# Head norms in a six-layer kernel: two tiles' means and spreads issued side by side on two halves of TensorE's array, and modulation blocks in a changed order

## The chip, the cores and the metric

The kernel runs on one core of a Trainium2 chip. The metric is device time in microseconds of one execution. All matrix products are in f32; the trace shows each of them as two MATMUL records (two passes over the moving operand), so "x4" in a row of the trace is two matmuls.

## What is computed

A chain of transformer layers on one sequence of 512 tokens (model width 1024), with a context of 256 tokens beside it. The first two layers (A/B and C/D) mix several kinds of attention; the next four have modulated norms, a mixer each and an MLP. What matters here is that queries and keys are normalised head by head before attention, and that the four later layers are modulated by vectors made from a condition:

```python
def rms_norm(z, g):
    zf = z.astype(jnp.float32)
    y = zf * lax.rsqrt(jnp.mean(zf * zf, axis=-1, keepdims=True) + NORM_EPS)
    return (y * g.astype(jnp.float32)).astype(z.dtype)
...
    qa = apply_rope(rms_norm(heads(qa, A_HEADS), a_qk_norm[0]), cos, sin)
    ka = apply_rope(rms_norm(heads(ka, A_KV_HEADS), a_qk_norm[1]), cos, sin)
...
def ada_mods(vec, w, b):
    m = jax.nn.silu(vec) @ w + b
    return [mi[..., None, :] for mi in jnp.split(m, N_MOD, axis=-1)]
```

## The kernel before, in words

Activations lie transposed: 128 features on the partitions, tokens along the free axis (512 for the sequence, 256 for the context). A stage of kind "project" walks over blocks of weights. A block is 2 MB, lies in one of three slots of `ring`, and is loaded on the SP queue in a fixed order: block b waits until block b-3 has been used (`freed_by`). For each tile of a block TensorE makes K/128 matmuls (L1395), ScalarE or VectorE takes the result out of PSUM, and then the list `t.after` of that tile is played: side steps that every engine plays in the same order, each doing its own part. So the order of all work is written out by hand in `after` lists.

A head norm (class `Heads`, one job for up to ten tiles) is made of such side steps. A tile holds 128 features, two heads of 64 (or four of 32). `square` (ScalarE, L1944) squares the tile into one of two buffers; the next square into the same buffer waits until `mean` has read it. `mean` (TensorE, L1422) multiplies the squares with a constant 128x22 matrix: each tile adds its two rows to one PSUM bank of 22 rows. After the last tile `sd` takes the root (ScalarE, L1952) and the reciprocal (VectorE, L2402). `spread` (TensorE, L1433) multiplies the 22 rows with a 22x128 constant, which copies a tile's rows back over its 128 partitions, into one of two banks; VectorE multiplies the tile by it (L2414). `swap` (TensorE, L1450) permutes features for the rotation, which VectorE (L2428, L2432) and GpSimd finish.

A modulation block is a 2 MB block of `in_ada_w` in the same ring ("ride"). VectorE sums it over its rows, weighted with the condition (L2277, L2281: 16 instructions for two conditions, 8 for one), into the buffer `partial`. One ride later TensorE adds up the partitions with matmuls of one column (`modulation`, L1355, 8 matmuls for two conditions), and VectorE adds the bias (`mods`, L2264). `ride(a)` is called by TensorE and by VectorE at the end of each group of tiles: it finishes the pending block, then takes a. Twelve blocks belong to a layer. In the C/D stage one group rides block X just before two groups that have weights but no tiles (`cmp_w`), and the group behind these, columns 1536 to 2048, rides another, called Y here.

Of the kernel before, what the change touches and what calls it, by code (L numbers as in the profile page):

```python
# [21 lines left out]
P = 128  # L22
D = 1024
KD = D // P
S = 512
C = 256
ST = S // P
HD = 64
# [27 lines left out]
PAIR_TILES, PAIR_ROWS = 11, 22  # L56
CD_PAIR_TILES = 8
QUAD_TILES, QUAD_ROWS, LAT_ROWS = 3, 12, 2
# [32 lines left out]
def head_norm_constants(tiles, rows, segments):  # L91
# [7 lines left out]
    return np.concatenate([mean.reshape(P, -1), spread.reshape(P, -1)], 1)  # L99


def constants():
    pos = np.arange(S)
    out = {}
# [24 lines left out]
    out["hn_pair"] = head_norm_constants(PAIR_TILES, PAIR_ROWS, [(0, 64), (64, 128)])  # L129

    mean, spread = np.zeros((P, 3, LAT_ROWS), np.float32), np.zeros((P, 3, P), np.float32)
    for i, (row, n) in enumerate(((0, 256), (0, 256), (1, 128))):
        mean[:, i, row], spread[row, i] = 1.0 / n, 1.0
    out["hn_cd"] = np.concatenate([head_norm_constants(QUAD_TILES, QUAD_ROWS, [(32 * j, 32 * j + 32) for j in range(4)]),
# [69 lines left out]
class Heads:  # L204


    def __init__(self, tiles, n, consts, rows, parts, swap, cos, sin, wk, mean, spread, turn, counts):
        self.tiles, self.n, self.consts, self.rows, self.parts = tiles, n, consts, rows, parts
# [3 lines left out]
        self.rs = wk[0:rows, 2 * S:2 * S + n]  # L212
# [5 lines left out]
        self.normed = [i for i, t in enumerate(tiles) if t[1] is not None]  # L218
# [10 lines left out]
def build_program(nc, dram, out_dram, stages_kept=10000):  # L229
    ctx = ExitStack()  # L230
    with ctx:
# [200 lines left out]
        def residual_halves(src, op, arg, normed, rides=0, **kw):  # L432
# [22 lines left out]
            return stage("project", groups=groups, sums_tile=groups[3][1][2], **kw)  # L455
# [17 lines left out]
        hn_t = reserve(PAIR_TILES * (PAIR_ROWS + P))  # L473
# [22 lines left out]
        def pair_constants(i, hn_t=hn_t):  # L496
            a = PAIR_TILES * PAIR_ROWS
            return (hn_t[:, i * PAIR_ROWS:(i + 1) * PAIR_ROWS], hn_t[0:PAIR_ROWS, a + i * P:a + (i + 1) * P])
# [3 lines left out]
        def heads(tiles, n, consts, rows, parts, swap=None, cos=None, sin=None, wk=None, mean=3, spread=(4, 5),  # L502
                  turn=(6, 7)):
            return Heads(tiles, n, consts, rows, parts, swap, cos, sin, wk, mean, spread, turn, hn_counts)
# [4 lines left out]
        for c0 in range(0, 2560, 512):  # L509
# [4 lines left out]
                          S, pair_constants, PAIR_ROWS, P, *rope)  # L514
# [8 lines left out]
        qk_heads = heads([(d, g, ab_list[i]) for i, (d, g) in enumerate(qk_data)], S, pair_constants, PAIR_ROWS, P, *rope)  # L523
# [4 lines left out]
        for i in range(10):  # L528
            ab_list[i].after.insert(0, ("square", qk_heads, i))
            ab_list[i + 1].after.append(("mean", qk_heads, i))  # L530
        ab_list[10].after.append(("sd", qk_heads, 0))
        for i in range(0, 10, 2):
            for j in (i, i + 1):
                ab_list[12 + i // 2].after.append(("spread", qk_heads, j))
                if i >= 2:
                    ab_list[12 + i // 2].after.insert(-1, ("swap", qk_heads, j - 2))
# [122 lines left out]
        hn_mean, hn_spread = reserve(CD_PAIR_TILES * PAIR_ROWS), reserve(CD_PAIR_TILES * P)  # L659
        hn_cd = reserve(QUAD_TILES * (QUAD_ROWS + P) + 3 * (LAT_ROWS + P))  # L660
# [19 lines left out]
        def pair_constants2(i):  # L680
            return hn_mean[:, i * PAIR_ROWS:(i + 1) * PAIR_ROWS], hn_spread[0:PAIR_ROWS, i * P:i * P + P]

        def quad_constants(i):
            a = QUAD_TILES * QUAD_ROWS
            return hn_cd[:, i * QUAD_ROWS:(i + 1) * QUAD_ROWS], hn_cd[0:QUAD_ROWS, a + i * P:a + i * P + P]

        def lat_constants(i):
            a = QUAD_TILES * (QUAD_ROWS + P)
            b = a + 3 * LAT_ROWS
            return hn_cd[:, a + i * LAT_ROWS:a + (i + 1) * LAT_ROWS], hn_cd[0:LAT_ROWS, b + i * P:b + i * P + P]  # L690
# [60 lines left out]
        cd_group(b, tiles[0:1], True)  # L751
        cd_group(b, tiles[1:])
# [7 lines left out]
        def job_of(data, consts, rows, at=None, n=S, table=None, swap=None):  # L760
            cos, sin = (None, None) if table is None else (table[:, 0:n], table[:, n:2 * n])
            return heads([(d, g, None if t is None else cd_list[t]) for d, g, t in data], n, consts, rows, P, swap, cos, sin,
                         head_wk)

        lat = job_of([(CQ[:, 0], V("qlat_g")[:, 0:1], 4), (CQ[:, 1], V("qlat_g")[:, 1:2], 5), (CKV[:, 0], V("kvlat_g"), 6)],
                     lat_constants, LAT_ROWS)
        swap_t, swap_q = rope_t[:, 2 * S:2 * S + P], rope_q[:, 2 * S:2 * S + P]
        qc = job_of([(QC[:, t], V("qc_g"), 8 + t) for t in range(4)], pair_constants2, PAIR_ROWS, table=rope_t, swap=swap_t)
        nope = job_of([(QU[:, t], dgain[:, 0:1], 12 + t) for t in range(4)]
                      + [(KU[:, t], dgain[:, 1:2], 18 + t) for t in range(4)], pair_constants2, PAIR_ROWS)  # L770
        quad = job_of([(QR[:, q], dgain[:, 2:3], 16 + q) for q in range(2)] + [(KR[:, 0], dgain[:, 3:4], 26)],
                      quad_constants, QUAD_ROWS, table=rope_q, swap=swap_q)
        ksw = job_of([(KS[:, 0], V("ks_g"), 32), (KW[:, 0], V("kw_g"), 33)], pair_constants2, PAIR_ROWS, table=rope_t,
                     swap=swap_t)
        kct = job_of([(KCT[:, 0:NCMP], V("kc_g"), None)], pair_constants2, PAIR_ROWS, n=NCMP, table=rope_c, swap=swap_t)
# [3 lines left out]
        for i in range(18, 26):  # L779
# [7 lines left out]
        after(11, ("spread", lat, 2), ("square", qc, 3), ("mean", qc, 2))  # L787
        after(12, ("mean", qc, 3), ("sd", qc, 0), ("square", nope, 0))
        after(13, ("square", nope, 1), ("mean", nope, 0))
        after(14, ("square", nope, 2), ("mean", nope, 1))  # L790
        after(15, ("square", nope, 3), ("mean", nope, 2))
        after(16, ("mean", nope, 3), ("spread", qc, 0), ("spread", qc, 1))
        after(18, ("square", nope, 4), ("swap", qc, 0), ("spread", qc, 2), ("swap", qc, 1), ("spread", qc, 3))
# [5 lines left out]
        after(25, ("square", quad, 1), ("mean", quad, 0))  # L799
        after(26, ("mean", quad, 1), ("square", quad, 2), ("spread", nope, 0), ("spread", nope, 1))  # L800
# [6 lines left out]
        after(33, ("swap", quad, 2), ("masked", quad, 2), ("square", ksw, 1), ("mean", ksw, 0))  # L807
        after(34, ("mean", ksw, 1), ("sd", ksw, 0), ("compress", None, 0))
# [5 lines left out]
        a = PAIR_TILES * PAIR_ROWS  # L814
        cd_stage = stage("project", groups=cd_groups, split=cd_norm, banks=3, freed=cmp_freed, loads=[
            (rope_t, dram["rope_ab"]), (rope_q, dram["rope_quad"]), (hn_mean, dram["hn_pair"][:, 0:CD_PAIR_TILES * PAIR_ROWS]),
            (hn_spread, dram["hn_pair"][:, a:a + CD_PAIR_TILES * P]), (hn_cd, dram["hn_cd"]),
# [2056 lines left out]
```

## Time and profile before

| | |
|---|---|
| time of three runs | 4119.92 us median (4116.33 to 4126.5) |
| the profiled execution's own time | 4117.78 us |
| its span, first to last instruction | 4115.9 us |
| TensorE busy | 3968.0 us, 96% of the span, 16604 matmul records |
| VectorE busy | 1756.9 us (43%) |
| ScalarE, GpSimd busy | 931.2 us (23%), 505.6 us (12%) |
| mean granted TensorE clock | 0.979 |

Two microseconds of the profiled time lie around the span. A row of the timeline gives start, duration, engine, line, what is written from what, the number of records merged into it, and in brackets the idle time ahead and what ended it. Records overlap a little, so the price of a piece of work is read as the start of the next row minus its own start.

### The profile page before, as it was taken

What the parts mean: (1) busy time and instruction counts of PE and PEld (TensorE: products, weight loads), DVE (VectorE), ACT (ScalarE), POOL (GpSimd) and SP (SyncE); (2) the same over time, 40 slices, a digit from 0 to 9 for tenths busy, and PEclk for the clock granted to TensorE, in tenths of its full rate; (3) what the DMA queues carried; (4) which work ended last, traced back from release to release, by engine and by line L of the source; (5) the groups of instructions that cost most, each with busy time, mean ns of one, the idle gap of its engine ahead of it and who ended that gap; (6) DMA issues with size and microseconds to landing.
All of it is one profiled execution on the core that took longest, in us unless ns stands there. A gap on an engine that the chain in (4) does not pass through costs nothing.

```text
span 4115.9 us, 42009 instructions
## 1 busy us (share of the span) xinstructions
PE 3968.0 (96%) x16604; PEld 2678.8 (65%) x16604; DVE 1756.9 (43%) x3123; ACT 931.2 (23%) x2130; POOL 505.6 (12%) x414
## 2 busy tenths in 40 slices
PE   9999989999999999999999899999999999999997
PEld 4358346544554556656545468888658888668886
DVE  2654454732574311112010465655574656224343
ACT  1142213621353211100010352011313101212020
POOL 1001000000000000000010332111342111111121
PEclk8999989999999999999999999999999999999999
DMA  3112323020100232322121313444112454112221
GB/s 127 62 42 85 115 82 114 1 76 21 44 1 10 71 122 83 111 94 96 68 72 41 97 32 123 165 174 131 63 41 80 151 179 143 67 57 87 82 82 41
DMA packets 226914, 343.03 MB, mean 83 GB/s; under 512 B 32225, under 2 KB 100353, under 8 KB 226689
## 3 DMA queue, kind: packets, MB, share of 16 engines
q1 hardware_dynamic: 202064, 322.44, 22.8%
q0 software_dynamic: 6816, 10.01, 1.2%
q10 hardware_dynamic: 17840, 7.91, 0.7%
q8 instruction: 134, 2.20, 0.2%
q14 instruction: 60, 0.48, 0.0%
HBM read 334.66 MB, written 4.06 MB: 82 GB/s over the span
## 4 chain that ended last, share of the span: by engine, by line
PE 73%; DVE 3%; POOL 1%; ACT 1%; issue 1%; DMA 0%; ACTq 0%; DVEq 0%; POOLq 0%
PE psum L1623 28%; PE psum L1395 28%; PE psum L1576 5%; PE psum L1580 3%; PE psum L1747 2%; PE psum L1694 2%; PE psum L1724 1%; PE psum L1492 1%; POOL arena L2758 1%; PE psum L1355 1%; DVE small L2578 1%; ACT arena L2064 1%; PE psum L1433 0%; PE psum L1422 0%; DVE psum L2574 0%
## 5 line engine op out<-in xcount | busy, mean ns | idle before, releaser
L1395 PE MATMUL psum<-H,ring 128*128 128x512 f32 (+1 forms) x3248 | 1160.4, 517 | 22.8 <-DMA ring<-in_cd_in 7.6
L1395 PEld LDWEIGHTS psum<-H,ring 128*128 128x128 f32 x3248 | 619.4, 192 | 541.4 <-issue 487.8
L1623 PE MATMUL psum<-arena,ring 128*128 128x256 f32 x1536 | 342.8, 380 | 2.8 <-ACT arena L1861 2.8
L2281 DVE SCALAR_TENSOR_TENSOR arena<-ring,cond,arena 128x512 f32<-128x512 f32 x448 | 320.5, 752 | 8.0
L1623 PEld LDWEIGHTS psum<-arena,ring 128*128 128x128 f32 x1536 | 290.4, 190 | 44.0 <-ACT arena L1861 5.3
L2715 POOL TENSOR_TENSOR ring<-ring 128x1024 f32<-128x1024 f32 x48 | 159.6, 3324 | 791.0 <-DVE arena L2128 791.0
L1623 PE MATMUL psum<-arena 128*128 128x256 f32 x1152 | 256.3, 379 | 0.4
L1623 PEld LDWEIGHTS psum<-arena 128*128 128x128 f32 x1152 | 218.6, 190 | 30.3 <-ACT arena L1866 0.7
L2578 DVE TENSOR_REDUCE small<-psum 128x1 f32<-128x512 f32 (+7 forms) x352 | 186.8, 565 | 115.9 <-PE psum L1706 50.3
L1576 PE MATMUL psum<-arena,ring 128*128 128x512 f32 x512 | 225.5, 593 | 0.2 <-issue 0.2
L2264 DVE TENSOR_TENSOR mods<-psum,vec 128x4 f32<-128x4 f32 (+1 forms) x48 | 7.7, 160 | 480.3 <-PE psum L1355 479.4
L2052 ACT ACTIVATE arena<-psum,small 128x256 f32<-128x256 f32 (+7 forms) x320 | 183.7, 578 | 120.7 <-DVE small L2578 80.6
L1395 PE MATMUL psum<-CH,ring 128*128 128x256 f32 x928 | 208.6, 383 | 0.0
L1395 PEld LDWEIGHTS psum<-CH,ring 128*128 128x128 f32 x928 | 176.3, 191 | 41.1 <-issue 14.1
L1724 PE MATMUL psum<-ident,arena 128*128 128x128 f32 x984 | 152.0, 284 | 32.8 <-ACT arena L2064 20.9
L1816 ACT ACTIVATE arena<-psum 128x512 f32<-128x512 f32 (+1 forms) x116 | 61.1, 527 | 538.8 <-PE psum L1395 534.5
L1623 PE MATMUL psum<-H,ring 128*128 128x256 f32 x768 | 177.0, 383 | 5.2 <-issue 4.5
L1623 PE MATMUL psum<-CX,arena 128*128 128x256 f32 x768 | 175.0, 382 | 5.8 <-DVE CX L2148 5.8
L1623 PE MATMUL psum<-CH,ring 128*128 128x256 f32 x768 | 169.7, 379 | 0.0
L1576 PEld LDWEIGHTS psum<-arena,ring 128*128 128x128 f32 x512 | 96.7, 190 | 108.7 <-issue 107.4
L1623 PEld LDWEIGHTS psum<-CX,arena 128*128 128x128 f32 x768 | 146.9, 192 | 27.1 <-issue 6.9
L1623 PEld LDWEIGHTS psum<-H,ring 128*128 128x128 f32 x768 | 145.7, 191 | 25.4 <-issue 5.2
(230 smaller groups left out, 4667.2 us busy)
## 6 DMA issues: line engine op xcount, KB each, us to landing
ring<-in_mlp_w SPq DMA_DIRECT2D x64, 2048.0 KB, 8.8
ring<-in_ada_w SPq DMA_DIRECT2D x48, 2048.0 KB, 8.0
ring<-in_na_qkv SPq DMA_DIRECT2D x6, 2048.0 KB, 7.8
ring<-in_ab_in SPq DMA_DIRECT2D x5, 2048.0 KB, 7.8
ring<-in_cd_in SPq DMA_DIRECT2D x4, 2048.0 KB, 7.9
ring<-in_pw SPq DMA_DIRECT2D x8, 1024.0 KB, 6.9
ring<-in_at_qkv SPq DMA_DIRECT2D x3, 2048.0 KB, 8.5
ring<-in_ab_out SPq DMA_DIRECT2D x2, 2048.0 KB, 8.2
```

The costliest lines, as they stand in the source:

```text
L1395: last = nc.tensor.matmul(out, lhs, rhs, start=(k == 0), stop=(k == len(t.pairs) - 1))
L1576: last = nc.tensor.matmul(bank(m), w[:, k, P * m:P * m + P], hid[:, KD * kb + k, :], start=(kb == 0 and k == 0), stop=(kb == 3 and k == KD ...
L1580: last = nc.tensor.matmul(bank(4 + m // 2, C, C * (m % 2)), w[:, k, P * m:P * m + P], hidc[:, KD * kb + k, :], start=(kb == 0 and k == 0 a ...
L1623: last = nc.tensor.matmul(bank(at, HALF, HALF * m), w[:, i, P * m:P * m + P], x[:, i, :], start=(opens and m == 0 and i == 0), stop=(i == ...
L1694: last = nc.tensor.matmul(psum[:, at:at + k1 - k0], p["q"](g, qt * P, qt * P + P), p["k"](g, a * P + k0, a * P + k1), start=(m < 3), stop= ...
L1724: last = nc.tensor.transpose(psum[0:rows, c0:c0 + P], pair["probs"][g][:, k0:k0 + rows], ident[:, :])
L1747: last = nc.tensor.matmul(psum[HD * g:HD * g + HD, at + q0:at + q1], p["v"](g, of[0] if of else kt), chunk["turned"][0:p["krows"], kt, g, ...
L1816: nc.scalar.activation(t.dst, src, ACT.Copy).then_inc(act_took, 1)
L2052: nc.scalar.activation(pair["probs"][g][:, 0:nk + more], psum[:, off:off + nk + more], ACT.Exp, bias=small[:, c:c + 1], accum_out=small[:, ...
L2281: ins = nc.vector.scalar_tensor_tensor(partial[:, v, :], w[:, k, :], cond[:, k, v:v + 1], partial[:, v, :], ALU.mult, ALU.add)
L2578: nc.vector.tensor_reduce(small[:, c:c + 1], psum[:, off:off + nk], AX, ALU.max, negate=True).then_inc(negmax_ready, 1)
L2715: nc.gpsimd.tensor_tensor(a21, a11, a21, ALU.subtract).then_inc(s3_made, 1)
```

## The change

Means: the constant becomes 128x64 for every set of two tiles. Tile 2k writes partitions 0 to 63 of the mean bank, tile 2k+1 partitions 64 to 127, each half with its own start and stop of accumulation. Spreads: the constant is 64x128, and tile 2k reads rows 0 to 63, tile 2k+1 rows 64 to 127. The `after` lists issue the two means of a set, and the two spreads of a set, one behind the other, and both swaps ahead of both spreads. The three latent tiles (`lat`) all stay on the lower half. Modulation: the first group of the A/B output stage is split, so that its ride comes after two of its four tiles; groups without tiles no longer ride; the group of columns 1536 to 2048 no longer rides, so every later block moves up by one ride and layer 0's MLP takes one more; the gains of layer 0's second norm are made at the end of the attention output stage rather than in `prep`.

```diff
-    mean = np.zeros((P, tiles, rows), np.float32)
-    spread = np.zeros((P, tiles, P), np.float32)
-    for i in range(tiles):
+    sets = (tiles + 1) // 2
+    mean = np.zeros((P, sets, HD), np.float32)
+    spread = np.zeros((2, HD, sets, P), np.float32)
+    for i in range(sets):
         for j, (a, b) in enumerate(segments):
             mean[a:b, i, len(segments) * i + j] = 1.0 / (b - a)
-            spread[len(segments) * i + j, i, a:b] = 1.0
+            spread[:, len(segments) * i + j, i, a:b] = 1.0
...
+def head_norm_views(table, tiles, i):
+
+
+    sets, lo = (tiles + 1) // 2, HD * (i % 2)
+    at = sets * HD + i // 2 * P
+    return table[:, i // 2 * HD:(i // 2 + 1) * HD], table[lo:lo + HD, at:at + P], lo
...
-            return stage("project", groups=groups, sums_tile=groups[3][1][2], **kw)
+            sums_tile, parts = groups[3][1][2], []
+            for b, tiles, a in groups:
+
+                parts += [(b, tiles[0:2], a), (b, tiles[2:], None)] if a else [(b, tiles, None)]
+            return stage("project", groups=parts, sums_tile=sums_tile, **kw)
...
         for i in range(10):
             ab_list[i].after.insert(0, ("square", qk_heads, i))
-            ab_list[i + 1].after.append(("mean", qk_heads, i))
+            if i % 2:
+                ab_list[i + 1].after += [("mean", qk_heads, i - 1), ("mean", qk_heads, i)]
...
-        cd_group(b, tiles[0:1], True)
-        cd_group(b, tiles[1:])
+        cd_group(b, tiles)
...
-        after(19, ("square", nope, 5), ("mean", nope, 4))
-        after(20, ("square", nope, 6), ("mean", nope, 5), ("swap", qc, 2), ("swap", qc, 3))
-        after(21, ("square", nope, 7), ("mean", nope, 6))
-        after(22, ("mean", nope, 7), ("sd", nope, 0))
+        after(19, ("square", nope, 5))
+        after(20, ("mean", nope, 4), ("mean", nope, 5), ("square", nope, 6), ("swap", qc, 2), ("swap", qc, 3))
+        after(21, ("square", nope, 7))
+        after(22, ("mean", nope, 6), ("mean", nope, 7), ("sd", nope, 0))
...
-            stage("prep", layer=layer, needs=[(0, 0), (1, 0)] + ([(0, 1)] if with_ctx else [])
-                  + ([(1, 1)] if layer == 0 else []))
+            stage("prep", layer=layer, needs=[(0, 0)] + ([(1, 0)] if layer else []) + ([(0, 1)] if with_ctx else []))
...
-        wide(dram["at_o"], at_out, rides=1)
+        wide(dram["at_o"], at_out, rides=1, steps=[("gains", 0, [(1, 0), (1, 1)])])
...
-                    ride(a)
+                    if tiles:
+                        ride(a)
...
-                nc.tensor.matmul(bank(job.mean_bank, job.n)[0:job.rows], job.consts(k)[0],
-                                 job.squares[0:job.parts, job.q[i] % 2, 0:job.n], start=(i == job.normed[0]),
-                                 stop=(i == job.normed[-1])).then_inc(square_read, 1)
+                of, _, lo = job.consts(k)
+                nc.tensor.matmul(bank(job.mean_bank, job.n)[lo:lo + HD], of,
+                                 job.squares[0:job.parts, job.q[i] % 2, 0:job.n], start=lo not in job.lows[:k],
+                                 stop=lo not in job.lows[k + 1:]).then_inc(square_read, 1)
...
-                nc.tensor.matmul(bank(at, job.n)[0:job.parts], job.consts(job.normed.index(i))[1], job.rs, start=True,
+                _, of, lo = job.consts(job.normed.index(i))
+                nc.tensor.matmul(bank(at, job.n)[0:job.parts], of, job.rs[lo:lo + HD], start=True,
```

What the change does to the order of instructions is shown at three places (the line numbers after the change are some 12 to 15 higher for the same code). First TensorE in the A/B projection, behind the twelfth tile, before; L1433 is a spread, L1450 a swap:

```order
L1433 MATMUL psum<-arena 128x512 x2
L1395 MATMUL psum<-H,ring 128x512 x8
L1450 MATMUL psum<-arena 128x512
L1433 MATMUL psum<-arena 128x512
L1450 MATMUL psum<-arena 128x512
L1433 MATMUL psum<-arena 128x512
L1395 MATMUL psum<-H,ring 128x512 x8
```

The same place after the change, where L1448 is a spread and L1465 a swap:

```order
L1448 MATMUL psum<-arena 128x512 x2
L1407 MATMUL psum<-H,ring 128x512 x8
L1465 MATMUL psum<-arena 128x512 x2
L1448 MATMUL psum<-arena 128x512 x2
L1407 MATMUL psum<-H,ring 128x512 x8
```

The alternation of swap and spread has become two swaps and then two spreads. Second, VectorE at the start of the A/B output stage, before; L2310 takes a tile into X, L2277 and L2281 are the sum of the ridden block:

```order
L2310 TENSOR_TENSOR X<-psum,X 128x256 x4
L2277 TENSOR_SCALAR arena<-ring,cond 128x512 x2
L2281 SCALAR_TENSOR_TENSOR arena<-ring,cond,arena 128x512 x14
L2310 TENSOR_TENSOR X<-psum,X 128x256 x4
L2264 TENSOR_TENSOR mods<-psum,vec 128x8
L2310 TENSOR_TENSOR X<-psum,X 128x256 x2
```

And after:

```order
L2325 TENSOR_TENSOR X<-psum,X 128x256 x2
L2292 TENSOR_SCALAR arena<-ring,cond 128x512 x2
L2296 SCALAR_TENSOR_TENSOR arena<-ring,cond,arena 128x512 x14
L2325 TENSOR_TENSOR X<-psum,X 128x256 x2
L2279 TENSOR_TENSOR mods<-psum,vec 128x8
L2325 TENSOR_TENSOR X<-psum,X 128x256 x6
```

The sum starts after two tiles, and the block is finished after four tiles rather than after eight. Third, TensorE in the C/D stage around the groups without tiles, before; L1355 is the modulation (x16 there is two blocks in a row), L1422 a mean, L1529 the compression:

```order
L1450 MATMUL psum<-arena 128x512
L1422 MATMUL psum<-arena 22x512
L1355 MATMUL psum<-ones,arena 128x1 x16
L1395 MATMUL psum<-H,ring 128x512 x8
L1422 MATMUL psum<-arena 22x512
L1529 MATMUL psum<-arena,ring 128x62 x16
```

And after:

```order
L1465 MATMUL psum<-arena 128x512
L1367 MATMUL psum<-ones,arena 128x1 x8
L1407 MATMUL psum<-H,ring 128x512 x8
L1436 MATMUL psum<-arena 64x512 x2
L1544 MATMUL psum<-arena,ring 128x62 x16
```

The second modulation (block X) has left this place, and both means stand behind the next tile.

## Rows read from the trace of the kernel before

**Rows 1.** The page's part 1: busy time, share, instructions.

```profile
PE 3968.0 (96%) x16604; PEld 2678.8 (65%) x16604; DVE 1756.9 (43%) x3123; ACT 931.2 (23%) x2130; POOL 505.6 (12%) x414
```

**Rows 2.** Windows: stretch, its length, busy time by engine, PEclk, DMA share, GB/s.

```profile
250.00:331.00 81.00, 75.72 (x627) 46.94 (x625) 57.35 (x200) 52.53 (x171) 0.00 (x0) 1.00 0.08 27
```

**Rows 3.** All means by source line: records, durations, forms (rows*columns of weights).

```profile
L1422 PE MATMUL psum<-arena x104: 188/592/609, 48.1 to 1067.0; 128*22 128x512 f32 x70, 128*22 128x256 f32 x20, 128*2 128x512 f32 x6, 128*12 128x512 f32 x6
```

**Rows 4.** Timeline of TensorE, A/B projection: a mean, spreads, swaps.

```profile
158.66 1.04 PE L1422 MATMUL psum<-arena 128*22 128x512 f32 x2
159.62 0.70 PE L1395 MATMUL psum<-H,ring 128*128 128x512 f32 x1
...
181.59 1.98 PE L1433 MATMUL psum<-arena 22*128 22x512 f32 x4
183.49 7.13 PE L1395 MATMUL psum<-H,ring 128*128 128x512 f32 x16
190.47 1.02 PE L1450 MATMUL psum<-arena 128*128 128x512 f32 x2
191.42 1.12 PE L1433 MATMUL psum<-arena 22*128 22x512 f32 x2
...
194.57 1.98 PE L1395 MATMUL psum<-H,ring 128*128 128x512 f32 x4
```

**Rows 5.** Timeline of TensorE: indexer scores, two heads on the two row halves.

```profile
116.38 1.13 PE L1459 MATMUL psum<-arena 64*128 64x512 f32 x4
117.44 1.04 PE L1422 MATMUL psum<-arena 128*22 128x512 f32 x2
```

**Rows 6.** Timeline of TensorE: probabilities times values, two heads on the two column halves.

```profile
1150.54 2.81 PE L1747 MATMUL psum<-arena 128*64 128x256 f32 x24
1153.28 1.13 PE L1694 MATMUL psum<-arena 64*128 64x512 f32 x5
```

**Rows 7.** Timeline of TensorE, A/B output stage.

```profile
331.19 27.86 PE L1395 MATMUL psum<-H,ring 128*128 128x256 f32 x128 [1.03 <-issue]
358.89 1.84 PE L1355 MATMUL psum<-ones,arena 128*128 128x1 f32 x16
```

**Rows 8.** Timeline of VectorE, A/B output stage.

```profile
338.37 0.42 DVE L2310 TENSOR_TENSOR X<-psum,X 128x256 f32<-128x256 f32 x1 [2.93 <-PE psum L1395]
...
345.62 0.87 DVE L2277 TENSOR_SCALAR arena<-ring,cond 128x512 f32<-128x512 f32 x2
...
356.16 1.07 DVE L2310 TENSOR_TENSOR X<-psum,X 128x256 f32<-128x256 f32 x3
```

**Rows 9.** Windows on a later stage, where TensorE had waited for GpSimd.

```profile
3018.00:3021.00 3.00, 2.90 (x4) 1.35 (x5) 1.87 (x3) 0.00 (x0) 2.34 (x3) 0.50 0.54 210
3021.00:3024.00 3.00, 3.00 (x7) 1.25 (x6) 3.00 (x6) 0.00 (x0) 0.00 (x0) 0.76 0.00 0
```

**Rows 10.** Timeline of TensorE at that later stage.

```profile
3018.10 5.40 PE L1492 MATMUL psum<-arena 128*128 128x512 f32 x7 [5.44 <-POOL arena L2758]
```

**Rows 11.** Timeline of TensorE, C/D projection around the groups without tiles.

```profile
542.92 2.93 PE L1395 MATMUL psum<-H,ring 128*128 128x512 f32 x3 [3.42 <-DMA ring<-in_cd_in]
...
582.97 1.92 PE L1355 MATMUL psum<-ones,arena 128*128 128x1 f32 x16
595.22 3.57 PE L1355 MATMUL psum<-ones,arena 128*128 128x1 f32 x16 [10.33 <-DVE arena L2281]
602.92 2.08 PE L1395 MATMUL psum<-H,ring 128*128 128x512 f32 x2 [4.13 <-DMA ring<-in_cd_in]
```

**Rows 12.** Timeline of VectorE and of the SP queue at the same place.

```profile
584.93 0.17 DVE L2264 TENSOR_TENSOR mods<-psum,vec 128x8 f32<-128x8 f32 x1 [0.19 <-PE psum L1355]
...
595.20 0.37 SPq L1296 DMA_DIRECT2D ring<-in_cd_in  x1
```

**Rows 13.** Timeline of ScalarE and TensorE, C/D projection, tiles of the KV weights.

```profile
484.52 0.60 ACT L1816 ACTIVATE arena<-psum 128x512 f32<-128x512 f32 x1 [0.76 <-PE psum L1395]
485.15 0.63 ACT L1944 ACTIVATE arena<-arena 128x512 f32<-128x512 f32 x1
...
489.12 1.13 PE L1395 MATMUL psum<-ring,arena 128*128 128x512 f32 x2
```

More of the change, by code:

```diff
@@ L204, with __init__ @@
 class Heads:
-    def __init__(self, tiles, n, consts, rows, parts, swap, cos, sin, wk, mean, spread, turn, counts):
-        self.tiles, self.n, self.consts, self.rows, self.parts = tiles, n, consts, rows, parts
+    def __init__(self, tiles, n, consts, parts, swap, cos, sin, wk, mean, spread, turn, counts):
+        self.tiles, self.n, self.consts, self.parts = tiles, n, consts, parts
+        self.normed = [i for i, t in enumerate(tiles) if t[1] is not None]
+        self.lows = [consts(k)[2] for k in range(len(self.normed))]
+        self.rows = max(self.lows) + HD
         self.swap, self.cos, self.sin = swap, cos, sin
@@ L211, in __init__ @@
         self.squares = wk[:, 0:2 * S].rearrange("p (b s) -> p b s", b=2)
[L212 removed]
+        self.rs = wk[0:self.rows, 2 * S:2 * S + n]
         self.yn = wk[0:parts, 3 * S:5 * S].rearrange("p (b s) -> p b s", b=2)
@@ L496, in pair_constants, with heads @@
         def pair_constants(i, hn_t=hn_t):
-            a = PAIR_TILES * PAIR_ROWS
-            return (hn_t[:, i * PAIR_ROWS:(i + 1) * PAIR_ROWS], hn_t[0:PAIR_ROWS, a + i * P:a + (i + 1) * P])
+            return head_norm_views(hn_t, PAIR_TILES, i)
         hn_counts = dict(job=0, spread=0, rope=0)
-        def heads(tiles, n, consts, rows, parts, swap=None, cos=None, sin=None, wk=None, mean=3, spread=(4, 5),
-                  turn=(6, 7)):
-            return Heads(tiles, n, consts, rows, parts, swap, cos, sin, wk, mean, spread, turn, hn_counts)
+        def heads(tiles, n, consts, parts, swap=None, cos=None, sin=None, wk=None, mean=3, spread=(4, 5), turn=(6, 7)):
+            return Heads(tiles, n, consts, parts, swap, cos, sin, wk, mean, spread, turn, hn_counts)
         cos_t, sin_t, swap_t = rope_t[:, 0:S], rope_t[:, S:2 * S], rope_t[:, 2 * S:2 * S + P]
@@ L806, in build_program @@
               ("square", ksw, 0))
-        after(33, ("swap", quad, 2), ("masked", quad, 2), ("square", ksw, 1), ("mean", ksw, 0))
-        after(34, ("mean", ksw, 1), ("sd", ksw, 0), ("compress", None, 0))
+        after(33, ("swap", quad, 2), ("masked", quad, 2), ("square", ksw, 1))
+        after(34, ("mean", ksw, 0), ("mean", ksw, 1), ("sd", ksw, 0), ("compress", None, 0))
         after(35, ("compress", None, 1))
@@ L1000, in build_program @@
             made = at_list[t0:t0 + count]
-            job = heads([(t.dst, gain, t) for t in made], S if is_x else C, pair_constants3, PAIR_ROWS, P,
+            job = heads([(t.dst, gain, t) for t in made], S if is_x else C, pair_constants3, P,
                         *(at_rope if is_x else (None, None, None, work)))
@@ L1004, in build_program @@
                 t.after.insert(0, ("square", job, i))
-                at_list[t0 + i + 1].after.append(("mean", job, i))
+                if i % 2:
+                    at_list[t0 + i + 1].after += [("mean", job, i - 1), ("mean", job, i)]
             at_list[t0 + count].after.append(("sd", job, 0))
@@ L1009, in build_program @@
                 if is_x and i:
-                    here += [("swap", job, i - 2), ("spread", job, i), ("swap", job, i - 1), ("spread", job, i + 1)]
-                else:
-                    here += [("spread", job, i), ("spread", job, i + 1)]
+                    here += [("swap", job, i - 2), ("swap", job, i - 1)]
+                here += [("spread", job, i), ("spread", job, i + 1)]
             if is_x:
@@ L2320, in project @@
                             side[kind](job, i)
-                    ride(a)
+                    if tiles:
+                        ride(a)
                 for kind, job, i in st.get("steps", []):
```

87 lines of the change are left out of this document (41 added, 46 removed).

## The prediction

> **What bounds the kernel now.** I read the page's busy shares first: TensorE is busy 96% of the span and no other engine comes near half [rows 1]. So the time is the time of TensorE's instruction stream, and a microsecond taken out of it is a microsecond won, except where TensorE stands and waits at the next step anyway. The second thing to read is therefore the timeline of TensorE, for the price of each small matmul and for the brackets, the waits. A price is the start of the next row minus the own start. In a stream of full matmuls a record of 512 columns takes 0.436 us (16 records from 183.49 to 190.47) [rows 4], so a whole f32 matmul takes 0.87 us; one of 256 columns takes 0.43 us (128 records from 331.19 to 358.89, 0.216 each) [rows 7].
>
> **The means.** A mean between tiles costs 0.96 us (158.66 to 159.62) [rows 4]: it streams 512 columns though it fills 22 columns of the array, and 0.1 us is lost in changing over. There are 104 records, so 52 matmuls [rows 3]. By the new lists 46 of them form 23 sets of two (A/B 5, C/D 8, the later attention 10), 18 sets of 512 columns and 5 of 256; six stay alone. What does a set cost? The trace does not show a mean in 64 columns, but it shows two heads on the two column halves writing one bank: 24 records of 256 columns take 2.74 us (1150.54 to 1153.28) [rows 6]. One behind the other they would take 24 times 0.216, 5.2 us. So both halves run at once, with 0.14 us for the change at both ends. A set of 512 columns is then 0.87 + 0.14, 1.0 us, in place of two times 0.96. Gain 0.92 each, 16.6 us for 18; a set of 256 columns I take as half, 0.46, 2.3 us for 5 (an estimate). The bounds are nothing, if the halves do not overlap, and 0.96 each. Means together: **18.9 us**.
>
> **The spreads.** They pair up in the same 18 and 5 sets. Eleven of the 18 stood side by side already, four records from 181.59 to 183.49, 1.90 us. Seven (four in A/B, one in C/D, two later) alternate with swaps: swap, spread, swap, spread from 190.47 to 194.57, 4.10 us [rows 4]. After the change two spreads lie on the two row halves and write different banks. The nearest row is the indexer, two heads on the row halves, 512 columns, between full matmuls: 1.06 us for both (116.38 to 117.44) [rows 5]. A set side by side gains 1.90 - 1.06 = 0.84, eleven times 9.2 us. In an alternating set two swaps in a row cost 0.95 (190.47 to 191.42) [rows 4] plus 0.87 in the stream, 1.82, and with the spreads 2.88 in place of 4.10: 1.22 us, seven times 8.5. The five of 256 columns at half, 0.42, give 2.1. Together **19.8 us**. The bounds are again nothing, and one matmul of 0.95 each.
>
> The VectorE and ScalarE steps keep their number and lengths: a reciprocal or a root works over 64 or 128 partitions in place of 22, along the same 512 columns. I cost that at nothing.
>
> The Trainium skill speaks against the change at one point. Its page "TensorEngine Tiling (Array Packing)", section "Tiling Modes", says that changing the tiling mode drains the engine, while tiles of one mode run independently. By that rule each set would pay a drain going in and another coming out. The indexer's pair agrees that there is a cost and sizes it, 1.06 us against 0.87 for the stream; a lone mean pays 0.1 of it already.
>
> **What the gain runs into.** Four places give some back.
>
> First, weights that come late. After the spreads of the last two tiles of `nope` TensorE waits 3.42 us for a block that is only requested when a tile ahead of them has ended [rows 11]. The 0.84 us won there become waiting. Second, block X. Before, TensorE finished one block at 582.97, waited 10.33 us for VectorE's sum of X, finished X (595.22), and waited 4.13 us more for the weights of the next tile [rows 11]. These are requested at 595.20, when the sum of X frees their slot [rows 12]. The change takes the modulation of X away from there, and the wait with it seems to go. It does not: the next instruction is now the tile whose weights arrive at 602.9, and the sum of X starts no sooner, since VectorE was idle for only 0.19 us before it [rows 12]. One wait of about 18.8 us takes the place of two. The mean that stood ahead was under the cover of this wait and now stands behind it in a set, so that set gains nothing: 0.9 us off. And the modulation of X, done in the shadow of the load before, is done behind four tiles in the open: 1.8 us off, the length of such a row [rows 7]. Block Y leaves this stage and costs the same in the MLP.
>
> Third, the A/B output stage. Eight tiles of 256 columns take 27.7 us, so four take 13.85 and end at 345.04 [rows 7]. VectorE takes the second tile at 338.37 to 338.79 and then sums the ridden block, which lasts 10.54 us (345.62 to 356.16) [rows 8]. The sum ends at 349.3. TensorE's modulation now stands after the fourth tile and waits **4.3 us** for it. Before, it came after eight tiles, at 358.89, and waited for nothing. Queued behind it on TensorE is the whole rest of the stage. Such a wait lets the granted clock fall: after the 5.44 us wait ending at 3018.10 [rows 10] the clock reads 0.50 over 3 us and 0.76 over the next 3 [rows 9], that is 3 + 1.4 us at 1.2 in place of 2.4 GHz, half of which, **2.2 us**, is lost. I charge it once here; the wait around X had a low clock already.
>
> Fourth, the small tiles of the KV weights. A copy and a square take ScalarE from 484.52 to 485.78, some 1.3 us after a tile's end, and such a tile lasts 0.9 to 1.1 us [rows 13]. Two sets there ask for the second square right after the next tile: 0.45 us of waiting each, 0.9 us.
>
> The three ridden changes elsewhere (a block more in layer 0's MLP, the gains moved, smaller tables) lie under tiles of 7 us each; if the cover of the extra sum were gone it would show as up to 10 us there, but a group of an MLP lasts far longer than the sum.
>
> **The sum.** 18.9 + 19.8 = 38.7. Off: 0.8 + 0.9 + 1.8 + 4.3 + 2.2 + 0.9 = 10.9. Net 27.8 us. The profiled execution's own time is 4117.8, so 4090.0; the median of the runs is 2.1 above it, so **4092 us**. Within 0.3%, 12.4 us, a measurement of this kernel tells nothing from no change; the forecast lies at 0.7%.
>
> **The rivals.**
> - The stalls are cheaper: no clock loss, the A/B wait hidden, and fewer drops of the clock behind thin matmuls. 38.7 less 4.4 is 34.3, with some 3 us of clock 37: 4083. For it: the sum does start earlier and frees its slot earlier. Against: TensorE reaches the wait by count of tiles. 0.14.
> - The stalls are dearer, or each set pays 0.1 us of drain on top. What the first row of a set costs in excess of one matmul is 0.1 to 0.2 us in the rows, so a doubled drain is 46 times 0.1, 4.6 us, and a clock that stays low for some 10 us behind both waits another 5: 4102. By the skill's rule on changing modes this is the direction; the rows say its price is mostly contained. 0.16.
> - The means do not run side by side, since both halves add into one bank, and only the spreads gain: 27.8 - 18.9 = 8.9, so 4111, no change that can be told. Against: the values' matmuls do just that in one bank [rows 6]. 0.08.
> - Slower: the half-filled sets count as idleness for the clock. If each of 46 sets were followed by 3.4 us at half clock, 1.7 us lost each, 78 us would go, for 4170; it turns slower by 0.3% from 24 such drops on. Against: attention is full of half-array pairs, and its window shows a clock of 1.00 [rows 2]. 0.03.
> - The forecast: 0.59.
>
> **How the numbers follow.** The forecast's own range is 4086 to 4099. With the two cases beside it, down to all stalls free (4079) and up to the doubled price and half of the next case, the range is 4079 to 4108. Faster by over 0.3% means under 4107.5: forecast, cheap and dear stalls, less their tails: 0.87. Same: 0.10. Slower: 0.03.
>
> **What would show it.** The means' line should have 104 records as before, but TensorE's starts in a set some 0.01 us apart, and a set should cost 1.0 us to the next tile. A spread set should cost 1.06. In the A/B output stage a wait of about 4.3 us on VectorE's sum should stand after four tiles, followed by a lower clock. Around the compression one wait of some 19 us on the weights should replace the two. TensorE's busy time should fall by about 40 us and its idle time rise by some 10. The prediction is wrong if the starts in a set lie 0.9 us apart, if TensorE's idle time grows by more than 20 us, or if the clock drops behind the sets.

## The result and the profile after the change

The changed kernel takes 4088.6 us (median of four runs, 4084.55 to 4091.74), the kernel before 4120.01 us (median of four). The ratio is 0.9923, 95% interval 0.9908 to 0.9937: 31 us faster, against a forecast of 4092 us. The profiled execution took 4087.81 us, its span 4085.7 us, at a mean granted clock of 0.978 (0.979 before).

The page's part 1 of the kernel after, beside [rows 1]:

```profile
PE 3926.6 (96%) x16600; PEld 2671.4 (65%) x16604; DVE 1751.1 (43%) x3123; ACT 932.8 (23%) x2131; POOL 506.3 (12%) x414
```

TensorE's busy time fell by 41.4 us; the span less that busy time rose from 147.9 to 159.1 us, by 11.2. The forecast was -40 and +10.

Timeline of TensorE after, A/B projection, the places of [rows 4]. L1436 is a mean, L1448 a spread, L1465 a swap, L1407 the projection:

```profile
99.03 1.08 PE L1436 MATMUL psum<-arena 128*64 128x512 f32 x4
100.03 1.55 PE L1407 MATMUL psum<-H,ring 128*128 128x512 f32 x3
...
177.09 1.13 PE L1448 MATMUL psum<-arena 64*128 64x512 f32 x4
178.14 7.13 PE L1407 MATMUL psum<-H,ring 128*128 128x512 f32 x16
185.12 1.88 PE L1465 MATMUL psum<-arena 128*128 128x512 f32 x4
186.93 1.13 PE L1448 MATMUL psum<-arena 64*128 64x512 f32 x4
187.98 1.55 PE L1407 MATMUL psum<-H,ring 128*128 128x512 f32 x3
```

Read starts, not durations. The set of means costs 100.03 - 99.03 = 1.00 us, where a single mean cost 0.96 [rows 4]. The first two of its four records, seen alone, last 0.65 us together, where the mean record of this line lasts 0.62, so they start almost together:

```profile
99.03 0.65 PE L1436 MATMUL psum<-arena 128*64 128x512 f32 x2
```

A set of spreads costs 1.05 us, where two cost 1.90. Two swaps and two spreads take 2.86 us (185.12 to 187.98), where the alternating four took 4.10. All three are the forecast's numbers to 0.02 us (1.0, 1.06, 2.88).

Timeline of TensorE after, A/B output stage, beside [rows 7]; L1367 is the modulation:

```profile
320.87 14.05 PE L1407 MATMUL psum<-H,ring 128*128 128x256 f32 x64 [1.03 <-issue]
339.06 2.57 PE L1367 MATMUL psum<-ones,arena 128*128 128x1 f32 x16 [4.14 <-DVE arena L2296]
341.50 23.68 PE L1407 MATMUL psum<-H,ring 128*128 128x256 f32 x96
365.02 0.50 PE L1485 MATMUL psum<-mean_d,arena 128*128 128x1 f32 x4
```

Timeline of VectorE after, the same stage, beside [rows 8]; L2296 is the sum of the ridden block:

```profile
328.05 0.42 DVE L2325 TENSOR_TENSOR X<-psum,X 128x256 f32<-128x256 f32 x1 [2.93 <-PE psum L1407]
328.39 0.87 DVE L2292 TENSOR_SCALAR arena<-ring,cond 128x512 f32<-128x512 f32 x2
329.18 9.83 DVE L2296 SCALAR_TENSOR_TENSOR arena<-ring,cond,arena 128x512 f32<-128x512 f32 x14
338.93 0.74 DVE L2325 TENSOR_TENSOR X<-psum,X 128x256 f32<-128x256 f32 x2
```

The wait of 4.14 us stands behind four tiles (64 records), as forecast (4.3). Before, eight tiles (128 records) and the modulation followed each other without a bracket; the rows behind it, before:

```profile
360.59 7.15 PE L1395 MATMUL psum<-H,ring 128*128 128x256 f32 x32
367.58 0.50 PE L1470 MATMUL psum<-mean_d,arena 128*128 128x1 f32 x4
```

Windows after, the granted clock behind this wait (length, busy time by engine, PEclk, DMA share, GB/s):

```profile
341.50:344.50 3.00, 3.00 (x8) 2.46 (x9) 0.17 (x1) 0.00 (x0) 0.00 (x0) 0.50 0.00 0
344.50:348.00 3.50, 3.50 (x12) 2.83 (x12) 0.05 (x1) 0.00 (x0) 0.00 (x0) 0.64 0.00 0
348.00:351.00 3.00, 3.00 (x16) 2.64 (x15) 0.38 (x1) 0.42 (x1) 0.72 (x1) 1.00 0.00 0
```

Behind the wait TensorE runs at 1.2 GHz (0.50) and then returns to 2.4. These two windows lose 3.0 x 0.50 + 3.5 x 0.36 = 2.8 us, and the modulation ahead of them, 2.44 us from start to next start against 360.59 - 358.89 = 1.70 before, another 0.7 (the clock reads 0.74 from 339.0 to 341.5). The stage from its first tile to the `mean_d` row lasts 365.02 - 320.87 = 44.15 us; the same stretch before lasted 367.58 - 331.19 = 36.39. So it lost 7.8 us: 4.14 of waiting, 3.5 by the clock.

Timeline of TensorE after, C/D projection, the places of [rows 11, 13]; the rows are the two sets of means between the small KV tiles (each with the row behind it), the late weights, the modulation ahead of the long wait, the tile and the set of means behind it, and the modulation of X:

```profile
474.75 1.64 PE L1436 MATMUL psum<-arena 128*64 128x512 f32 x4
476.32 1.98 PE L1465 MATMUL psum<-arena 128*128 128x512 f32 x4
...
479.95 1.64 PE L1436 MATMUL psum<-arena 128*64 128x512 f32 x4
481.52 2.84 PE L1407 MATMUL psum<-ring,arena 128*128 128x512 f32 x6
...
527.20 16.04 PE L1407 MATMUL psum<-H,ring 128*128 128x512 f32 x32 [4.87 <-DMA ring<-in_cd_in]
...
566.06 1.92 PE L1367 MATMUL psum<-ones,arena 128*128 128x1 f32 x16 [0.93 <-DVE arena L2444]
585.96 8.81 PE L1407 MATMUL psum<-H,ring 128*128 128x512 f32 x16 [17.98 <-DMA ring<-in_cd_in]
594.70 1.08 PE L1436 MATMUL psum<-arena 128*64 128x512 f32 x4
...
630.35 1.92 PE L1367 MATMUL psum<-ones,arena 128*128 128x1 f32 x16 [1.66 <-DVE arena L2444]
```

One wait of 17.98 us stands where 10.33 and 4.13 stood. From the modulation ahead of it to the tile behind it are 585.96 - 566.06 = 19.90 us, before 602.92 - 582.97 = 19.95: nothing is won or lost between the two. A set among the KV tiles costs 1.57 us rather than 1.00, since the second square is late: inside each of the two TensorE waits 0.4 us for ScalarE's square (L1959). The SP queue shows why the long wait ends when it does (the issue of these weights after the change):

```profile
578.28 0.37 SPq L1308 DMA_DIRECT2D ring<-in_cd_in  x1
```

VectorE's sum of X after:

```profile
568.90 9.36 DVE L2296 SCALAR_TENSOR_TENSOR arena<-ring,cond,arena 128x512 f32<-128x512 f32 x14
```

It ends at 578.26. From the issue to the tile are 7.7 us, as before (595.20 to 602.92) [rows 11, 12]. The load has not become slower; it is still asked for only when VectorE has summed X.

### The profile page after: what moved, and what is told of

Read it like the earlier page. It is cut to its first block, busy times and chain, and to the rows that moved or that the text cites. A ratio compares the mean times of both kernels' runs of the same rounds, so it can differ in the third digit from the quotient of the medians.

```text
span 4085.7 us, 42004 instructions
## 1 busy us (share of the span) xinstructions
PE 3926.6 (96%) x16600; PEld 2671.4 (65%) x16604; DVE 1751.1 (43%) x3123; ACT 932.8 (23%) x2131; POOL 506.3 (12%) x414
## 4 chain that ended last, share of the span: by engine, by line
PE 73%; DVE 3%; POOL 1%; ACT 1%; issue 1%; DMA 0%; DVEq 0%; ACTq 0%; POOLq 0%
PE psum L1638 28%; PE psum L1407 28%; PE psum L1591 5%; PE psum L1595 3%; PE psum L1762 2%; PE psum L1709 2%; PE psum L1739 1%; PE psum L1507 1%; POOL arena L2774 1%; PE psum L1367 1%; DVE small L2594 1%; ACT arena L2079 1%; DVE psum L2590 0%; DVE arena L2609 0%; PE psum L1665 0%
## 5 line engine op out<-in xcount | busy, mean ns | idle before, releaser
L1407 PE MATMUL psum<-H,ring 128*128 128x512 f32 (+1 forms) x3248 | 1160.5, 517 | 38.1 <-DMA ring<-in_cd_in 22.8
L1407 PEld LDWEIGHTS psum<-H,ring 128*128 128x128 f32 x3248 | 622.0, 193 | 554.8 <-issue 483.9
L2296 DVE SCALAR_TENSOR_TENSOR arena<-ring,cond,arena 128x512 f32<-128x512 f32 x448 | 320.5, 754 | 8.0
L1407 PE MATMUL psum<-CH,ring 128*128 128x256 f32 x928 | 206.7, 380 | 0.0
L1407 PEld LDWEIGHTS psum<-CH,ring 128*128 128x128 f32 x928 | 175.2, 190 | 39.9 <-issue 14.3
```

The costliest lines, as they stand in the source:

```text
L1407: last = nc.tensor.matmul(out, lhs, rhs, start=(k == 0), stop=(k == len(t.pairs) - 1))
L2296: ins = nc.vector.scalar_tensor_tensor(partial[:, v, :], w[:, k, :], cond[:, k, v:v + 1], partial[:, v, :], ALU.mult, ALU.add)
```

## The experiments

Every kernel was timed beside the kernel before on one chip; ratios are to it, over all runs, and need not be the quotient of two medians. Kernels are compared with each other by their ratios. The first four shared a chip (before 4117.78 us, median of 17), the last two another (4125.55, median of 11).

**1. The same order, without the two halves.** All tiles of a set write columns 0 to 63 and read rows 0 to 63; nothing moves in the order. The tables of constants are other ones, so that the head norms it computes aren't the reference's; instructions and shapes are the changed kernel's.

```diff
...
-    sets, lo = (tiles + 1) // 2, HD * (i % 2)
-    at = sets * HD + i // 2 * P
-    return table[:, i // 2 * HD:(i // 2 + 1) * HD], table[lo:lo + HD, at:at + P], lo
+    at = HD + 4 * (tiles - 1)
+    m0 = 4 * (tiles - 1) - (4 if tiles == QUAD_TILES else 2) * i
+    return table[:, m0:m0 + HD], table[0:HD, at + i * P:at + (i + 1) * P], 0
...
```

> The changed kernel with the same order of instructions on every engine, but every tile's mean in columns 0 to 63 and every spread in rows 0 to 63, so that the two of a set share one half. Theory (the halves run at once): each set pays its second matmul again, 0.87 us for 512 columns and 0.43 for 256, that is 18 x 2 x 0.87 + 5 x 2 x 0.43 = 35.6 us, less about 1 us that lies under the waits in the C/D stage: 4088.6 + 34.5 = 4123 us. A set of means should take 1.9 us to the next tile in place of 1.0. Rival (the gain comes from the new order, the wider constants, or the clock): the time stays near 4089.

Measured: 4122.58 us (12 runs), ratio 1.0011, interval 1.0002 to 1.0019. Groups by form, of this kernel and then of the changed one (records | busy, mean ns | idle before):

```profile
L1448 PE MATMUL psum<-arena 64*128 64x512 f32 x82 | 41.0, 617 | 1.6 <-DVE arena L2418 1.6
L1436 PE MATMUL psum<-arena 128*64 128x512 f32 x82 | 40.5, 611 | 0.0
```

```profile
L1436 PE MATMUL psum<-arena 128*64 128x512 f32 x82 | 25.9, 618 | 0.0
L1448 PE MATMUL psum<-arena 64*128 64x512 f32 x82 | 25.9, 639 | 2.7 <-DVE arena L2418 2.7
```

And the timeline of one set of means in this kernel, at the place of the 99.03 row:

```profile
102.04 1.93 PE L1436 MATMUL psum<-arena 128*64 128x512 f32 x4
103.90 2.41 PE L1407 MATMUL psum<-H,ring 128*128 128x512 f32 x5
```

A set on one half costs 1.86 us, on two halves 1.00. The same 82 records have nearly the same mean duration, but on two halves they cover 15 us less of TensorE's time on each line: they overlap, and no record became shorter. Between the two ratios, 1.0011 and 0.9923, lie 36 us, with some 7 of uncertainty: that is what the halves are worth, as expected (34.5), and the forecast's terms for them (18.9 and 19.8, of which 2.7 is the mere order of swaps and spreads, seven times 4.10 less 1.90 less 1.82) make 36.0. The order with the modulation part but without the halves gives no gain. The rival, 4089 us, falls.

**2. The norms alone.** The changed kernel with the modulation blocks as before (A/B output group whole, X ahead of the groups without tiles, every group rides).

```diff
...
-                    if tiles:
-                        ride(a)
+                    ride(a)
...
```

> The head norms of the changed kernel with the modulation blocks, the gains and prep as before. Theory: the modulation part of the change costs time (the wait of 4.1 us in the A/B output stage with 3.5 us of lower clock behind it, and 1.8 us for block X's modulation in the open), so without it the time is 4088.6 - 9.4 = 4079 us. Rival (the modulation order gives part of the gain, since one ride less stands in the C/D stage): slower than the changed kernel, 4092 or more.

Measured: 4083.36 us (4073.3 to 4084.77, 5 runs), ratio 0.9907, interval 0.9893 to 0.9922: 38 us faster than before by the ratio, 34 by the medians. Against the whole change that is 7 us better, with some 8 of uncertainty, so the times alone don't show that it is faster than the whole change. The rival, 4092 us or more, falls.

**3. The modulation part alone.** The kernel before with exactly those edits.

```diff
...
-                    ride(a)
+                    if tiles:
+                        ride(a)
...
```

> The kernel before with only the modulation part of the change (split group, no ride of groups without tiles, one ride less, gains moved). Theory: 4120.0 + 9.4 = 4129 us, with a wait of about 4 us on VectorE's sum after four tiles of the A/B output stage. Rival (one wait less around the compression): 4110 to 4120 us.

Measured: 4133.86 us (4132.16 to 4135.31, 5 runs), ratio 1.0037, interval 1.0024 to 1.0051. By itself this half of the change costs 15 us by the ratio, 16 by the medians, with some 5 of uncertainty, where 9.4 were expected; the rival, a gain or nothing, falls. Timeline of TensorE in this kernel, the A/B output stage and the weights behind X:

```profile
350.44 3.58 PE L1357 MATMUL psum<-ones,arena 128*128 128x1 f32 x16 [4.14 <-DVE arena L2284]
...
612.35 10.18 PE L1397 MATMUL psum<-H,ring 128*128 128x512 f32 x16 [18.08 <-DMA ring<-in_cd_in]
```

Both waits are those of the changed kernel to 0.1 us. They belong to the modulation part and have nothing to do with the norms. What makes it cost more than the 9.4 stays open.

**4. The A/B output group whole again.** All else as changed.

```diff
-            sums_tile, parts = groups[3][1][2], []
-            for b, tiles, a in groups:
...
-            return stage("project", groups=parts, sums_tile=sums_tile, **kw)
+            return stage("project", groups=groups, sums_tile=groups[3][1][2], **kw)
```

> The changed kernel with the A/B output stage's first group whole again, so that its ride comes after four tiles and is finished after eight. Theory: the wait and the low clock behind it go, 4088.6 - 7.8 = 4081 us. Rival (the late sum only moves the wait to a later place, or the clock falls there anyway): 4087 to 4090 us.

Measured: 4082.03 us (4076.11 to 4085.17, 5 runs), ratio 0.9910, interval 0.9897 to 0.9923, which is 5 us better than the changed kernel's 0.9923 where 7.8 were expected. Timeline of TensorE, the same stage:

```profile
324.24 27.86 PE L1403 MATMUL psum<-H,ring 128*128 128x256 f32 x128 [1.03 <-issue]
351.94 1.84 PE L1363 MATMUL psum<-ones,arena 128*128 128x1 f32 x16
```

Eight tiles run through and the block finished behind them waits for nothing, as in [rows 7]. The clock reads 1.00 from 320 to 367 us. In the trace the 7.8 us are back (second line of the table below); the timed ratios say 5, with some 8 of uncertainty, which alone would not tell the theory from its rival (no gain).

**5. X one stage later.** Experiment 4, and the KC group (columns 512 to 1024) takes no block; X is taken behind the first tile of columns 1536 to 2048, where Y used to be.

```diff
-        cd_group(b, tiles, True)
+        cd_group(b, tiles)
...
-        cd_group(b, tiles)
+        cd_group(b, tiles[0:1], True)
+        cd_group(b, tiles[1:])
```

The first pair of lines is the KC group, the second the group of columns 1536 to 2048; minus is experiment 4.

> The changed kernel with the A/B output group whole (as in no_split, 4082.0 us), and with the modulation of the rest moved: the projection group of KC issues no block between its tiles, and the blocks of X come behind the first tile of the group of columns 1536 to 2048, a stage later than in the changed kernel. The slot of the ring that this group's weights need is then freed by the blocks of KC, and not by VectorE's last sum. Theory (the 17.98 us wait on the weights is the late freeing of that slot, and nearly all of it is owed to where X's blocks stand): the wait falls to about 8 us, 10 us are won, 4072 us. Rival 1: the weights are late whatever frees the slot (SP's queue, the link's rate): 17 to 18 us of waiting in one or two pieces, 4082 us. Rival 2: the wait falls, but the thin matmuls of X's sum stand behind it alone and lower the granted clock for some microseconds: 4075 to 4078 us.

Measured: 4072.26 us (4066.55 to 4075.7, 4 runs), ratio 0.9877, interval 0.9864 to 0.9890: the fastest of all. In ratio it is 0.0033, 13.6 us, better than experiment 4, and 19 us better than the changed kernel, with some 8 of uncertainty on each; 10 and about 17 were expected. Timeline of TensorE in this kernel:

```profile
564.86 1.92 PE L1364 MATMUL psum<-ones,arena 128*128 128x1 f32 x16 [0.93 <-DVE arena L2441]
572.01 9.75 PE L1404 MATMUL psum<-H,ring 128*128 128x512 f32 x16 [5.23 <-DMA ring<-in_cd_in]
```

And of its SP queue:

```profile
563.10 0.37 SPq L1305 DMA_DIRECT2D ring<-in_cd_in  x1
```

The weights are now asked for at 563.10, when the tile ahead has used the slot, 3.7 us before TensorE comes for them (564.86 + 1.92), where the changed kernel asks 10.3 us after (578.28 against 567.98). The wait is 5.23 us in place of 17.98, and from the modulation to the tile are 7.15 us in place of 19.90. VectorE's sum of X (596.74 to 606.10) lies under the tiles behind. Rival 1 falls. Of rival 2's clock loss the timed result shows nothing; in the trace the clock does read 0.50 from 572 to 576 us and 0.89 from 576 to 582, 2.7 us lost behind the wait, and the mean granted clock is 0.978, that of the changed kernel. This is the version that beats both kernels.

**6. The means apart.** The changed kernel with every mean at its old place in the order, still on alternating halves; spreads in sets.

```diff
...
-            if i % 2:
-                ab_list[i + 1].after += [("mean", qk_heads, i - 1), ("mean", qk_heads, i)]
+            ab_list[i + 1].after.append(("mean", qk_heads, i))
...
```

> The changed kernel with the means of two tiles at their old places, each before its own tile's squares, a projection block or more apart, though still on different halves of the array; the spreads stand in sets of two as in the changed kernel. Theory (two sets of means that are adjacent and on different halves run in the time of one: 17 sets of 512 columns won about 0.9 us each, 5 of 256 about 0.45): 17 to 18 us more than the changed kernel, 4106 us. Rival (the gain of the means is little, since mean and projection hide each other anyway, and the spreads carry it): no more than 5 us over the changed kernel, 4089 to 4094 us.

Measured: 4105.05 us (4099.69 to 4114.51, 6 runs), ratio 0.9962, interval 0.9949 to 0.9974. Against the changed kernel's 0.9923 that is 0.0039, 16 us, with some 8 of uncertainty; 17 to 18 were expected, and the rival, 5 us at most, falls. Groups by form:

```profile
L1434 PE MATMUL psum<-arena 128*64 128x512 f32 x82 | 43.9, 617 | 0.4 <-ACT arena L1957 0.4
L1446 PE MATMUL psum<-arena 64*128 64x512 f32 x82 | 25.9, 639 | 1.6 <-DVE arena L2416 1.6
L1434 PE MATMUL psum<-arena 128*64 128x256 f32 x20 | 6.5, 404 | 0.0
```

The means cover 43.9 us instead of 25.9 and the twenty records of 256 columns 6.5 instead of 3.3; the spreads are unchanged. A mean that stands alone on its half costs 1.00 us (timeline of this kernel):

```profile
577.62 1.07 PE L1434 MATMUL psum<-arena 128*64 128x512 f32 x2
578.62 1.61 PE L1365 MATMUL psum<-ones,arena 128*128 128x1 f32 x13
```

That is what a set of two costs when adjacent. The theory holds: the means' term is about 16 us, and apart on two halves they gain nothing over single means on one (0.96 before).

**Where the traces stand, stage by stage.** For each kernel the start of the same row less its start before, in us (negative: earlier). The rows are the first bf16 matmul of the A/B and of the C/D attention, the first matmul that reads `sd_rstd` and `mean_d` behind each of them, the first transpose of the later attention, and the end. The profiled execution of the norms alone was the fastest of its kernel, 10 us under its median.

| stretch ends at (before) | norms alone | mods alone | changed | whole group | X later | means apart | one half |
|---|---|---|---|---|---|---|---|
| A/B attention, 251.5 | -11.0 | 1.1 | -10.3 | -6.9 | -6.7 | -4.4 | 1.2 |
| A/B output, 371.5 | -11.0 | 9.7 | -2.6 | -6.9 | -6.7 | 3.3 | 8.9 |
| C/D attention, 680.6 | -26.5 | 12.7 | -18.6 | -16.8 | -29.2 | -5.9 | 12.4 |
| layer 0, norm, 907.6 | -28.2 | 12.7 | -17.2 | -23.0 | -28.6 | -12.1 | 10.6 |
| later attention, 1094.9 | -44.8 | 12.8 | -33.7 | -39.5 | -46.1 | -20.2 | 6.5 |
| end, 4115.9 | -44.7 | 16.1 | -30.2 | -35.9 | -42.2 | -18.2 | 11.2 |

Behind 1094.9 nothing moves by more than 5 us. The table also shows how far a single trace can be read. The changed kernel and the one with the group whole issue the same instructions up to the A/B attention and stand 3.4 us apart there; in C/D, again with the same instructions, the one gains 16.0 us between the second line and the third and the other 9.8. Most of that is the clock: added up over the windows of low clock in which TensorE works, that stretch loses some 13 us before, 9 in the changed kernel and 16 with the group whole (estimates from PEclk times length). Without it the two gain 12 us alike, which is what the forecast has for this stretch (11.9). Where this table and the timed ratios differ, the ratios count.

## Why the prediction was right, point by point

**Two means in the time of one.** Right, with the size: forecast 1.0 us a set and 18.9 us in all, less 0.9 for the set under cover, which is 18.0; taking the adjacency away cost 16 us, give or take 8. None of the signs of being wrong came: the starts in a set lie far less than 0.9 us apart, idle time grew by 11.2 us and not 20, and from 970 to 1050 us, where sets of the later attention stand, the clock reads 1.00.

**Spreads.** Right: 1.05 and 2.86 us against 1.06 and 2.88. With the means apart the change still gains 0.0038, 16 us, all stalls included, where 27.8 - 18.0 = 9.8 would follow from the sum; the interval is 5 us to either side, and the sum lacked a gain of the clock (below). The Trainium skill, page "TensorEngine Tiling (Array Packing)", section "Tiling Modes", says that changing the tiling mode drains the engine. The trace agrees that a set costs something beyond its one matmul's time, and the price is small: 1.00 - 0.87 = 0.13 us for means and 1.05 - 0.87 = 0.18 us for spreads, as the rows before had it.

**The A/B wait.** Right in place, cause and length (4.14 for 4.3). What follows it was sized too small: the clock term was 2.2 us and measured 3.5, since it left out that the clock also falls under the modulation itself, right behind the wait (2.44 us where it cost 1.70 before). Stage by stage the two terms together cost 7.8 us, where 6.5 were forecast.

**Block X.** Right that the 10.33 us wait would not go but be taken over by the weights. The wait is 17.98 us for "about 18.8"; the missing 0.9 stands one row earlier, as a wait of 0.93 us for VectorE ahead of the modulation (566.06), where the mean used to stand. Experiment 5 shows the cause: the slot. The change moved the matmuls of X away but not the sum, which frees it.

**Late weights behind `nope`.** Right in kind: 3.42 us of waiting became 4.87, so this wait took back 1.45 us of what the norms had won ahead of it, against the 0.8 charged.

**KV tiles.** 1.57 - 1.00 = 0.57 us a set, twice; 0.45 was forecast. A wait of 0.44 us for ScalarE that one mean had there before (494.43) is gone, which the forecast did not count.

**What the sum lacked.** The later attention (907.6 to 1094.9) gained 16.5 us in the changed kernel and in the one with the norms alone, and its ten sets were forecast at 13.9. The kernel with all tiles on one half gained 4.1 us there (10.6 to 6.5 in the table) with no overlap at all. Two stretches of reduced clock of the kernel before are gone in it. Windows of the kernel before:

```profile
1004.00:1021.00 17.00, 16.50 (x58) 10.97 (x56) 4.84 (x3) 2.92 (x8) 2.50 (x2) 0.90 0.00 1
1050.00:1063.00 13.00, 12.51 (x42) 7.80 (x41) 5.75 (x5) 2.28 (x5) 2.50 (x2) 0.88 0.01 1
```

And of the kernel on one half, the same places:

```profile
1000.00:1025.00 25.00, 24.50 (x75) 12.92 (x74) 5.72 (x5) 4.73 (x9) 0.74 (x1) 1.00 0.00 0
1025.00:1075.00 50.00, 49.50 (x164) 28.71 (x163) 18.90 (x24) 7.55 (x16) 6.74 (x6) 1.00 0.12 43
```

17.00 us at 0.90 and 13.00 at 0.88 are 1.7 + 1.6 = 3.3 us, and two alternating sets there give 0.38 each by their order: 4.1 us. The other 12.4 are the overlap, less three waits that grew by 0.4 us each. The modulation part did not take the drops away: alone it still has them (0.90 from 1017 to 1034 us, 0.87 from 1063 to 1076). Nor did the means' place: with the means apart they are gone as well. Which of the two that are left did it, the order of spreads and swaps or the constants that are 64 wide for all, was not tried. The timed runs point the same way: on one half the kernel is at 1.0011 and with the modulation part alone at 1.0037, 11 us apart, with some 7 of uncertainty, where the order alone was priced at 2.7. Fewer drops of the clock stood only in the forecast's first rival, at 3 us.

**The net.** The sum had 27.8 us, the profiled execution won 30.2 and the medians 31.4. By the stretches of the table the forecast is -10.3, +6.5, -11.9, 0, -13.9 and, for the block that moved into layer 0's MLP, +1.8; the changed kernel has -10.3, +7.7, -16.0, +1.4, -16.5 and +3.5. The two stretches that won more than forecast owe it to the clock, some 4 us in C/D, which the same instructions did not get in the kernel with the group whole, and 3.3 in the later attention; the others lost 1.2, 1.4 and 1.7 us more than forecast. So the terms are right in kind and mostly in size, while that the total is met to 3 us is in part luck: errors of 1 to 4 us went both ways. Over the whole span the clock gave nothing: 0.979 of 4115.9 us before and 0.978 of 4085.7 after leave 86 and 90 us lost.

What stays open is the price of the modulation part: alone it costs 15 us, on top of the norms 7 us (0.9923 against 0.9907), with 5 to 8 us of uncertainty on each. The A/B part of it is the same in both traces (8.6 and 7.7 us between the first two lines of the table); in C/D it costs 3.0 us alone and gains 0.5 with the norms. Behind 1094.9 the six kernels that have it lose 2.0 to 4.7 us and the norms alone nothing. In the changed kernel 1.8 of these 3.5 us lie in layer 0's MLP, where one more block is finished; the rest was not traced to a cause.

## What to carry to other kernels

In this kernel two f32 matmuls that fill half of the columns, or half of the rows, run in little more than the time of one if they stand next to each other on opposite halves (1.00 and 1.05 us, 1.86 on one half); assigned to halves but apart they gain nothing (1.00 us each). So change the order and the table together, and price the set by a pair of the same shape that the trace already has. A wait that disappears from one engine's list is won only if whatever it covered was requested early enough: ask what frees the slot of the next load, and move that step rather than the one that was seen waiting. A wait can cost more than its length: behind 4.14 us of waiting what followed lost 3.5 us more to the lower clock.

## What the runs showed of the hardware

One program does not get the same clock in each of its executions: the 17 runs of the kernel before on one chip lie between 4112.65 us at a mean clock of 0.982 and 4128.87 at 0.976. A single stretch can make up a good part of that. Windows of 16 us at the same place of the C/D attention, of the changed kernel and then of the one with the group whole, whose instructions are the same there:

```profile
784.00:800.00 16.00, 15.71 (x96) 10.55 (x94) 6.80 (x35) 7.26 (x31) 0.00 (x0) 0.60 0.00 1
```

```profile
785.00:801.00 16.00, 15.27 (x130) 9.47 (x128) 11.17 (x46) 9.79 (x39) 0.00 (x0) 1.00 0.00 2
```

One runs 96 records at a mean clock of 0.60, the other 130 at 1.00: 16.00 x 0.40 = 6.4 us. That is most of what the lines "C/D attention" and "layer 0, norm" of the table differ by (-18.6 to -17.2 against -16.8 to -23.0). The stretch is missing in two of the eight traces (group whole and means apart). A difference of 6 us between two single profiles says nothing until the clock of their windows is laid side by side.
